# Query and key projections of the forgetting attention by Strassen's scheme in fp32, with bias spreads and key turns in one run among the products

## The chip, the cores and the metric

The kernel runs as one program on one core of a Trainium2 chip. The metric is the device time of one execution in microseconds; the figure that counts is the median over several executions. TensorE (PE in the rows) multiplies, VectorE (DVE), ScalarE (ACT) and GpSimd (POOL) do the elementwise work, and SyncE (SP) runs no arithmetic: it waits, reads indices and issues transfers, one after the other in program order. Each engine executes its own instruction list strictly in order, and the lists meet in semaphores.

## The reference, cut to what matters

One inference step of a one-layer decoder. A prompt of 1024 tokens and a sample group of 8 x 8 = 64 tokens go through the same weights, so that every projection is over 1088 tokens of 1024 channels. The part that is changed is the projection `fq`, `fk` below; beside it stand the load of `cache_fox_logf` through the page table, and the projections of the dilated heads (`dq`, `dk`, `dv`).

```python
def mixer_inputs(xn, pos, w_in, b_fgate):
    z = xn @ w_in
    fq, fk, fv, fz, dq, dk, dv, gate_fox, gate_dil = jnp.split(z, cuts, axis=-1)
    logf = jax.nn.log_sigmoid(fz.astype(jnp.float32) + b_fgate.astype(jnp.float32))
...
def fox_prompt(q, k, v, logf):            # 8 heads of 64, blocks of 128 queries
    c = jnp.cumsum(logf, axis=1)
    s = jnp.einsum('bqhd,bkhd->bhqk', qb, k) * (dh ** -0.5)
    s = s + cb[..., None] - c_keys[:, :, None, :]
    p = jax.nn.softmax(jnp.where(causal, s, -jnp.inf), axis=-1)
...
kv_past = cache_fox_kv[page_table, l]      # sample group: 16 pages of 128 rows for each of 8
lf_past = cache_fox_logf[page_table, l]
```

Everything is fp32. fk also leaves as an output, token by token.

## The kernel before, in words

`xnT` holds the normalised input with channels on partitions: 8 blocks (`KD`) of 128 channels by 1088 tokens. The weights `wK` and `wQ` hold 8 x 512 columns each. Two heads share 128 output columns; there are four such pairs, j = 0 to 3, in stages `p0` to `p3` of the plan. `foxpair_pe` makes, for a pair, the keys and the queries in chunks of 512, 288 and 288 tokens (`CHUNKS`): 8 matmuls into one of two PSUM banks, which ScalarE copies out to `KT` or `QT` (`foxpair_act`, semaphore `copied`). Each pair also needs four spreads of the cumulated log forgets over the partitions (512 columns each, "bias") and nine transposes of its keys ("turns", L561), which `foxpair_dve` copies from a third bank into one of two buffers `ktok`; POOL stores them (L637), and a buffer is taken again once its store has landed (`kstored0`, `kstored1`).

The order of each engine's list is not written down as such. Every stage is a generator that yields the planned time of its next step, and `weave` merges the generators of an engine by these times; the plan is the table `PLAN`, which the change leaves alone:

```python
PLAN = dict(
    norm1=(1.8, 73.8), v=(10, 82), p0=(82, 112), sums=(92, 93),
    p1=(112, 174), a0=(114, 176), p2=(174, 236), a1=(178, 238), p3=(236, 298), a2=(240, 300),
    d0=(298, 440), a3=(302, 372), b0=(380, 480), d1=(440, 580), b1=(500, 612), d2=(580, 715), b2=(640, 752),
```

The attention of pair j (`a0` to `a3`; scores L707, turns L735, values L724) is so laid among the projections of pair j + 1. `d0`, `d1` and `d2` are the projections of the three groups of dilated heads (`dilproj_pe`, matmuls L1068, turns L1085), with the attention `b0` of the first group (L838, L850, L863) beside `d1`. Their weights, 3 MB for a group in three transfers, are issued by SyncE in `dilproj_sp` (L1038), then a table of rotations (L1045). The past log forgets come by 128 transfers of 4 KB, whose addresses SyncE reads out of the page table one by one:

```python
for n in range(NB * NPG):                      # lf_sp, L1610 to L1615
    yield at("p0")(0) + 0.3 * n
    pid = sp.value_load(ptab[0:1, n:n + 1], min_val=0, max_val=N_POOL - 1)
    sp.dma_start(lf_raw[n:n + 1, :], lf_pool[bass.ds(pid, 1), :, :]...).then_inc(s_lf, 16)
```

They are transposed on TensorE in `p3` (L547), and `suffix_dve` sums them.

Of the kernel before, what the change touches and what calls it, by code (L numbers as in the profile page):

```python
# [22 lines left out]
P = 128  # L23
# [149 lines left out]
def build(nc, I, O, TAB):  # L173

    with ExitStack() as ctx:
# [225 lines left out]
        fp = sems("foxproj", "v_computed v_copied z_in z_act lf_out computed copied k_turned k_kept summed sums_out "  # L401
# [108 lines left out]
        PAIR_AT = [[sum(0.15 if kind == "bias" else 1.0 for kind, _ in units[0:x]) / 6.6 for x in range(PAIR + 1)]  # L510
                   for units in PAIR_UNITS]

        def foxpair_pe(pe, j):
            now = at(f"p{j}")
            for x, (kind, n) in enumerate(PAIR_UNITS[j > 0]):
                q, start = PAIR * j + x, PAIR_AT[j > 0][x]
                if kind == "bias":
                    yield now(start)
                    if j == 0 and n == 0:
                        pe.wait_ge(fp["sums_out"], 1)  # L520
                    pe.wait_ge(fp["copied"], q - 1)
                    pe.matmul(banks[q % 2], ident[:, 2 * j + n // 2:2 * j + n // 2 + 1].to_broadcast([P, P]),
                              cT[:, n % 2 * 512:(n % 2 + 1) * 512], start=True, stop=True).then_inc(fp["computed"], 1)
                    continue
                w, (c0, cw) = (wK if kind == "k" else wQ), CHUNKS[n]
                for k in range(KD):
                    yield now(start + k / KD / 6.6)
                    if k == 0 and q == 0:
                        pe.wait_ge(fp["wk_in"], 16)
                        pe.wait_ge(*nth(n1, "kept", 2 * TT))  # L530
                        conv_rows_pe(pe)
                    if k == 0 and q == 3:
                        pe.wait_ge(fp["wq_in"], 16)
                    if k == 0 and q >= 2:
                        pe.wait_ge(fp["copied"], q - 1)
                    last = pe.matmul(banks[q % 2][:, 0:cw], w[:, k, j * P:(j + 1) * P], xnT[:, k, c0:c0 + cw],  # L536
                                     start=(k == 0), stop=(k == KD - 1))
                last.then_inc(fp["computed"], 1)
                if kind == "k" and j == 3 and n < 2:
                    yield now(start + 0.95 / 6.6)  # L540
                    if n == 0:
                        pe.wait_ge(s_lf, 16 * NB * NPG)
                        pe.wait_ge(fp["k_kept"], 9)
                    else:
                        pe.wait_ge(fp["lf_kept"], 1)
                    for h in range(4):
                        last = pe.transpose(banks[2][:, h * P:(h + 1) * P], lf_raw[:, 4 * n + h::HF], ident)  # L547
                    last.then_inc(fp["lf_turned"], 1)
                if kind == "q":
                    g = 3 * j + n  # L550
                    yield now(start + 0.95 / 6.6)
                    pe.wait_ge(fp["copied"], PAIR * j + 3)
                    if g == 0:
                        pe.wait_ge(s_vec, 2)
                    else:
                        pe.wait_ge(fp["k_kept"], g)
                    if g == 9:
                        pe.wait_ge(fp["lf_kept"], 2)
                    for i in range(4 if n < 2 else 1):
                        t = 4 * n + i  # L560
                        last = pe.transpose(banks[2][0:rows_of(t), i * P:(i + 1) * P], KT[j % 2][:, t * P:t * P + rows_of(t)], ident)  # L561
                    last.then_inc(fp["k_turned"], 1)

        def foxpair_act(act, j):
            now = at(f"p{j}")
            for x, (kind, n) in enumerate(PAIR_UNITS[j > 0]):
                q = PAIR * j + x
                yield now(PAIR_AT[j > 0][x + 1])
                act.wait_ge(fp["computed"], q + 1)
                if x == 0 and j == 0:  # L570
                    act.wait_ge(*nth(n1, "kept", 2 * TT))
                    act.wait_ge(s_clear, 4)
                if x == 0 and j >= 2:
                    act.wait_ge(*nth(att_fox, "scored", att_fox["scored_by"][NQ * (j - 1) - 1]))
                    act.wait_ge(*nth(att_fox, "drained", att_fox["scored_by"][NQ * (j - 1) - 1]))
                    act.wait_ge(fp["k_turned"], 3 * (j - 1))
                src = banks[q % 2]
                if kind == "bias":
                    act.activation(bias_p[j % 2][:, n // 2, n % 2 * 512:(n % 2 + 1) * 512], src, ACT.Copy).then_inc(fp["copied"], 1)
                    continue  # L580
                c0, cw = CHUNKS[n]
                if kind == "k":
                    act.activation(KT[j % 2][:, c0:c0 + cw], src[:, 0:cw], ACT.Copy).then_inc(fp["copied"], 1)
                else:
                    m = min(cw, S - c0)
                    last = act.activation(QT[j % 2][:, c0:c0 + m], src[:, 0:m], ACT.Copy, scale=-QSCALE)
                    if m < cw:
                        for a in range(2):
                            last = act.activation(qbF[64 * a:64 * a + 64, j, :, 8 * a:8 * a + 8],
                                                  src[64 * a:64 * a + 64, m:cw].rearrange("p (b c) -> p b c", c=NS),  # L590
                                                  ACT.Copy, scale=QSCALE)
                    last.then_inc(fp["copied"], 1)

        def foxpair_dve(dve, j):
            now = at(f"p{j}")
            if j == 0:
                yield now(0.1)
                conv_rows_dve(dve)
            for n in range(2 if j == 3 else 0):
                yield now((n + 1.1) / 6.6)  # L600
                dve.wait_ge(fp["lf_turned"], n + 1)
                dve.tensor_copy(lf_all.rearrange("s p (b h) -> s h b p", h=HF)[:, 4 * n:4 * n + 4, :, :],
                                banks[2].rearrange("s (h b p) -> s h b p", h=4, b=NB)).then_inc(fp["lf_kept"], 1)
            for n in range(3):
                yield now(PAIR_AT[j > 0][PAIR_UNITS[j > 0].index(("q", n)) + 1])
                g, r = 3 * j + n, (P, P, SM)[n]
                dve.wait_ge(fp["k_turned"], g + 1)
                if g >= 2:
                    dve.wait_ge(fp[f"kstored{g % 2}"], 16 * (g // 2))
                w = 512 if n < 2 else P  # L610
                dve.tensor_copy(ktok[g % 2][0:r, 0:w], banks[2][0:r, 0:w]).then_inc(fp["k_kept"], 1)
# [319 lines left out]
        def mask_rows(dve, x):  # L931

            j, u = x // NQ, NQ - 1 - x % NQ
            if u == NQ - 1:
                dve.wait_ge(fp["copied"], PAIR * (j + 1))
            v = bias_p[j % 2][:, :, u * P:(u + 1) * P]
            dve.tensor_tensor(v, v, causal.unsqueeze(1).to_broadcast([P, 2, P]), ALU.add).then_inc(fp["masked"], 1)

        def fox_unit(x):
            j, u = x // NQ, NQ - 1 - x % NQ  # L940

            def add_ready(dve):
# [5 lines left out]
                W=(u + 1) * P, scores_ready=lambda pe: pe.wait_ge(fp["copied"], PAIR * (j + 1)), add_ready=add_ready,  # L948
# [74 lines left out]
        def dilproj_sp(sp, g):  # L1023
            yield at(f"d{g}")(0) - 40 if g else at("p3")(0.6)
            if g == 0:
                sp.wait_ge(s_foxout, FOXOUT)
                sp.wait_ge(fp["lf_out"], 1)
                sp.wait_ge(fp["computed"], 4 * PAIR - 3)
# [11 lines left out]
            if g == 0:  # L1040
                yield at("p3")(1)
                sp.wait_ge(fp["computed"], 4 * PAIR)
# [4 lines left out]
        def dilproj_pe(pe, g):  # L1047
# [29 lines left out]
        def dil_turn(pe, g, t):  # L1077
            s, z = dp[g]["s"], dp[g]["z"]
            pe.wait_ge(s["roped"], z["roped"] + t + 1)
            if g == 0 and t == 0:  # L1080
                pe.wait_ge(fp["k_kept"], 12)
            if g or t:
# [43 lines left out]
        def dilproj_act(act, g):  # L1126
            s, z = dp[g]["s"], dp[g]["z"]
            now = at(f"d{g}")
            for t in range(TT + 1):
# [3 lines left out]
                if t < TT:  # L1133
                    if t == 0:
                        yield now(1 / TT)
                        if g == 0:
                            act.wait_ge(fp["computed"], 4 * PAIR)
# [470 lines left out]
        def lf_sp(sp):  # L1608

            for n in range(NB * NPG):  # L1610
                yield at("p0")(0) + 0.3 * n
                if n == 0:
                    sp.wait_ge(s_ptab, 16)
                pid = sp.value_load(ptab[0:1, n:n + 1], min_val=0, max_val=N_POOL - 1)
# [157 lines left out]

        def suffix_dve(dve):
            yield at("p3")(0.5)
            dve.wait_ge(fp["lf_kept"], 2)
            dve.memset(lfs[:, NPG - 1, :], 0.0).then_inc(fb["suffix"], 1)
            for n, p in enumerate(range(NPG - 2, -1, -1)):
                yield at("p3")(0.5) + 4 * n
# [1698 lines left out]
```

## Time and profile before

| | |
|---|---|
| three executions | 2625.26, 2626.5, 2635.47 us, median 2626.5 us |
| profiled execution | 2628.53 us, its span 2626.7 us |
| TensorE busy | 2591.1 us, 99% of the span |
| VectorE, ScalarE, GpSimd busy | 1195.6, 521.2, 178.4 us |
| granted TensorE clock, mean | 0.997 |
| moved by DMA | 299.22 MB |

The span is that of one execution; 1.8 us of its time lie outside. Busy TensorE includes the tail of each matmul, which overlaps the next one, so that lengths are better read from the starts of consecutive rows. One fp32 matmul is recorded as two instructions, a transpose as one.

### The profile page before, as it was taken

To read this page: it belongs to the slowest core of one execution; us is meant where nothing else is said; L and a number is where in the kernel's file an instruction comes from. 1 tells how busy PE (TensorE), PEld (TensorE's weight loads), DVE (VectorE), ACT (ScalarE), POOL (GpSimd) and SP (SyncE) were. 2 spreads that over 40 slices of the span, in tenths; PEclk is the share of its full clock that TensorE was granted. 3 is DMA by queue.
4 is the path that set the end of the run, shared out by engine and by line. 5 is a ranking of instruction groups with operands and counts; after the bars stand their busy time and mean duration, and the time that the engine had idled before them with its cause. 6 is when DMAs were issued, how large, how long until landed. Compare 5 with 4: busy or idle time off the path is not lost.

```text
span 2626.7 us, 37785 instructions
## 1 busy us (share of the span) xinstructions
PE 2591.1 (99%) x14338; PEld 1821.2 (69%) x14338; DVE 1195.6 (46%) x2902; ACT 521.2 (20%) x1143; POOL 178.4 (7%) x284
## 2 busy tenths in 40 slices
PE   8999999999999999999999999999999999999999
PEld 7655656666656666676445886558888888888887
DVE  2155653332253333343553443355666666654432
ACT  2233323221202222121011112311211212110002
POOL 1000001232202222000000000000000000000000
PEclk9999999999999999999999999999999999999999
DMA  5000101100117888787215104433544452162101
GB/s 199 23 13 10 62 1 58 62 20 21 49 29 232 267 260 259 233 267 238 111 48 202 42 1 165 153 82 116 185 142 136 148 163 68 33 202 94 66 31 69
DMA packets 208474, 299.22 MB, mean 114 GB/s; under 512 B 20941, under 2 KB 145246, under 8 KB 207254
## 3 DMA queue, kind: packets, MB, share of 16 engines
q1 hardware_dynamic: 149462, 192.47, 22.5%
q10 hardware_dynamic: 42976, 89.26, 10.6%
q0 software_dynamic: 15856, 15.07, 2.3%
q8 instruction: 115, 1.88, 0.3%
q14 instruction: 65, 0.53, 0.1%
HBM read 270.43 MB, written 65.71 MB: 128 GB/s over the span
## 4 chain that ended last, share of the span: by engine, by line
PE 95%; DMA 2%; DVE 1%; ACT 1%; ACTq 1%; issue 1%; SPq 0%; DVEq 0%
PE psum L2853 22%; PE psum L3235 11%; PE psum L1068 10%; PE psum L2048 8%; PE psum L536 5%; PE psum L2136 4%; PE psum L2535 4%; PE psum L1424 3%; PE psum L2237 3%; PE psum L2056 3%; PE psum L707 3%; PE psum L724 2%; PE psum L2513 2%; PE psum L1440 2%; PE psum L1460 2%; PE psum L735 1%
## 5 line engine op out<-in xcount | busy, mean ns | idle before, releaser
L2853 PE MATMUL psum<-arena 128*128 128x272 f32 x2464 | 568.0, 394 | 1.2 <-DVE arena L2927 1.2
L2853 PEld LDWEIGHTS psum<-arena 128*128 128x128 f32 x2464 | 469.9, 191 | 98.6 <-issue 1.3
L3235 PE MATMUL psum<-arena 128*128 128x256 f32 (+1 forms) x1584 | 288.1, 356 | 0.0
L1068 PE MATMUL psum<-arena 128*128 128x512 f32 (+3 forms) x960 | 284.6, 458 | 0.0
L2048 PE MATMUL psum<-arena 128*128 128x368 f32 (+1 forms) x768 | 279.1, 475 | 0.9 <-DVE arena L1984 0.6
L3235 PEld LDWEIGHTS psum<-arena 128*128 128x128 f32 (+1 forms) x1584 | 252.4, 178 | 34.7 <-issue 3.2
L1068 PEld LDWEIGHTS psum<-arena 128*128 128x128 f32 (+1 forms) x960 | 150.2, 179 | 89.1 <-issue 78.3
L2048 PEld LDWEIGHTS psum<-arena 128*128 128x128 f32 x768 | 127.8, 190 | 52.0 <-issue 14.8
L2956 DVE TENSOR_TENSOR arena<-arena,psum 128x272 f32<-128x272 f32 (+2 forms) x330 | 111.8, 378 | 112.7 <-PE psum L2853 112.0
L1424 PEld LDWEIGHTS psum<-arena 128*128 128x128 f32 x848 | 105.0, 141 | 69.1 <-issue 46.3
L2977 DVE SCALAR_TENSOR_TENSOR arena<-arena 128x1024 f32<-128x1024 f32 x88 | 113.1, 1285 | 52.6 <-ACT arena L2879 51.1
L2877 ACT ACTIVATE arena<-arena 128x1024 f32<-128x1024 f32 x44 | 54.2, 1232 | 401.2 <-DVE arena L2956 401.2
L536 PE MATMUL psum<-arena 128*128 128x288 f32 (+1 forms) x384 | 132.4, 478 | 0.2
L1483 DVE COPY arena<-psum 128x512 f32<-128x512 f32 (+1 forms) x108 | 73.6, 682 | 128.0 <-PE psum L1424 127.8
L1424 PE MATMUL psum<-arena 128*128 128x128 f32 x848 | 127.5, 273 | 3.0 <-DMA arena<-in_cache_fox_kv 1.8
L3347 DVE TENSOR_TENSOR arena<-arena,psum 128x256 f32<-128x256 f32 (+1 forms) x128 | 46.6, 401 | 178.9 <-PE psum L3235 178.8
L2136 PE MATMUL psum<-arena 128*128 128x512 f32 x256 | 122.0, 596 | 0.0
L1490 ACT ACTIVATE arena<-psum 128x512 f32<-128x512 f32 (+1 forms) x108 | 63.6, 589 | 293.4 <-PE psum L1424 290.2
L2535 PE MATMUL psum<-arena 128*128 128x272 f32 x448 | 108.2, 392 | 0.0
L2056 PE MATMUL psum<-arena 128*128 128x352 f32 (+2 forms) x288 | 100.8, 457 | 0.0
L784 DVE CUSTOM_DVE_ANT_0 arena<-psum,arena 128x512 f32<-128x512 f32 (+3 forms) x128 | 65.2, 538 | 75.5 <-PE psum L707 75.3
L2237 PE MATMUL psum<-arena 128*128 128x512 f32 x224 | 98.0, 593 | 0.8 <-issue 0.8
(274 smaller groups left out, 2950.6 us busy)
## 6 DMA issues: line engine op xcount, KB each, us to landing
arena<-in_cache_fox_kv ACTq DMA_DIRECT2D x128, 256.0 KB, 4.7
arena<-in_cache_fox_kv SPq DMA_DIRECT2D x128, 256.0 KB, 5.0
out_win_s<-in_cache_win_kv ACTq DMA_DIRECT2D x8, 4080.0 KB, 15.0
arena<-in_w_up SPq DMA_DIRECT2D x44, 512.0 KB, 6.5
arena<-in_w_down SPq DMA_DIRECT2D x14, 1408.0 KB, 6.2
arena<-in_cache_win_kv SPq DMA_DIRECT2D x16, 1024.0 KB, 8.6
arena<-in_cache_mem_kv SPq DMA_DIRECT2D x16, 1024.0 KB, 6.3
out_y_p<-arena SPq DMA_DIRECT2D x20, 512.0 KB, 2.7
```

What stands on the lines that cost most here:

```text
L536: last = pe.matmul(banks[q % 2][:, 0:cw], w[:, k, j * P:(j + 1) * P], xnT[:, k, c0:c0 + cw], start=(k == 0), stop=(k == KD - 1))
L1068: last = pe.matmul(banks[c0 // 512][p0:p0 + r, 0:n], xn_tile(k, g, t), wD[g][:, k, w0:w0 + n], start=(k == 0), stop=(k == KD - 1))
L1424: last = pe.transpose(a["turn"][n % 2][:, x * P:(x + 1) * P], k, ident)
L2048: last = pe.matmul(banks[0][:, 0:cw], w[:, k, :], xnT[:, k, c0:c0 + cw], start=(k == 0), stop=(k == KD - 1))
L2056: last = pe.matmul(banks[1][:, 0:pw], w[:, 8 + k, :], oT[:, k, c0:c0 + pw], start=(k == 0), stop=(k == kn - 1))
L2136: last = pe.matmul(banks[h], lhs(k)[:, t * P:(t + 1) * P], w[h][:, k, :], start=(k == 0), stop=(k == KD - 1))
L2237: last = pe.matmul(mix_out(u), merged[:, ks, tok + t * P:tok + (t + 1) * P][:, k, :], wm[side][:, ws, :][:, k, :], start=(k == 0), stop=(k ...
L2535: last = pe.matmul(query_bank(n), w[:, k, :], r[:, k, XT4 * p:XT4 * p + XT4], start=(k == 0), stop=(k == 3))
L2853: last = pe.matmul(bank_of(j, x, p), w[:, k, :], r[:, k, Q4 * p:Q4 * p + Q4], start=(k == 0), stop=(k == 3))
L2956: last = dve.tensor_tensor(dst, dst if base is None else view(base), view(bank), ALU.add)
L2977: dve.scalar_tensor_tensor(out=tp, in0=up[:, tap:tap + S], scalar=w, in1=tp, op0=ALU.mult, op1=ALU.add).then_inc(done, 1)
L3235: last = pe.matmul(down_out(u)[p0:p0 + r, 0:n], hT(f)[:, tok + t * P:tok + t * P + r], slot[slots[c]][:, f - fa, c0:c0 + n], start=(f == f ...
```

## The change

With the channels in two halves and the tokens in two halves of 544, the keys and queries of a pair are a product of 2 x 2 blocks: weights (key, query) by channel halves, inputs (channel halves) by token halves. Strassen's scheme (in Winograd's form) makes it from 7 block products in place of 8. Each product is done in two parts of 272 tokens (p = 0, 1), with 4 matmuls of 272 columns each, in one of three banks that go round. The first product is copied out by ScalarE; the others are added by VectorE onto `KT`, `QT` and one intermediate (`onto`). VectorE also makes the input sums `k_t1` to `k_t4` once, and the weight sums of each pair. The four spreads and the nine key turns of the pair ahead now use the same three banks and stand behind the eighth product part; the key turns of pair 3 come behind all products. `k_t1` takes the place of `lf_all` and `lf_raw`: so the loop of the past log forgets moves behind the last product, their transposes into `d1`.

```diff
-        PAIR = 10
-        ks, qs, bs = [("k", n) for n in range(3)], [("q", n) for n in range(3)], [("bias", n) for n in range(4)]
-        PAIR_UNITS = (ks + qs + bs, ks + bs + qs)
+        QT2, QT4 = TOK // 2, TOK // 4
+        SUMS, COPIES = 16, 7
+        PRODUCTS = [("product", x, p) for x in range(7) for p in range(2)]
+        SPREADS = [("bias", n, 0) for n in range(4)]
+        K_TURNS = [("turn", n, 0) for n in range(3)]
+        PAIR_UNITS = [PRODUCTS + SPREADS]
+        PAIR_UNITS += [PRODUCTS[0:8] + SPREADS + K_TURNS + PRODUCTS[8:] for j in range(3)]
+        PAIR_UNITS += [K_TURNS]
...
+        k_t1, k_t2, k_t3 = [take(4 * QT2, a).rearrange("p (k t) -> p k t", k=4) for a in (B2 + 4 * TOK, f0 + 34432, f0 + 15872)]
...
+            w = (a11, s2, a12, a21, a22, s1, s4)[x]
+            return w[:, k, :], t4 if x == 4 else (k_b11, k_t2, k_b21, k_t3, None, k_t1, k_b22)[x][:, k, cols]
...
-                w, (c0, cw) = (wK if kind == "k" else wQ), CHUNKS[n]
-                for k in range(KD):
...
-                    last = pe.matmul(banks[q % 2][:, 0:cw], w[:, k, j * P:(j + 1) * P], xnT[:, k, c0:c0 + cw],
-                                     start=(k == 0), stop=(k == KD - 1))
+                if kind == "turn":
+                    yield pair_at(j, i)
+                    pe.wait_ge(*nth(qk, "summed", SUMS * j))
+                    pair_drained(pe, q - 3)
...
+                for k in range(4):
+                    yield pair_at(j, i) + (pair_at(j, i + 1) - pair_at(j, i)) * k / 4
...
+                        if q >= 3:
+                            pair_drained(pe, q - 3)
+                    w, r = pair_operands(j, x, k, p)
+                    last = pe.matmul(banks[q % 3][:, 0:QT4], w, r, start=(k == 0), stop=(k == 3))
...
+        def pair_weight_sums(dve, j):
...
+            dve.tensor_tensor(s1, a21, a22, ALU.add).then_inc(qk["s"]["w_sums"], 1)
...
+                    if g >= 2:
+                        dve.wait_ge(fp[f"kstored{g % 2}"], 16 * (g // 2))
+                    dve.tensor_copy(ktok[g % 2][0:r, 0:w], banks[q % 3][0:r, 0:w]).then_inc(fp["k_kept"], 1)
...
-            yield at(f"d{g}")(0) - 40 if g else at("p3")(0.6)
+            yield at(f"d{g}")(0) - 40 if g else at("p3")(0.9)
...
-                sp.wait_ge(fp["computed"], 4 * PAIR - 3)
+                sp.wait_ge(*nth(qk, "computed", unit_at(3, "product", 4, 1) + 1))
...
-                                pe.wait_ge(fp["copied"], 4 * PAIR - (0 if c0 else 1))
+                                pe.wait_ge(*nth(qk, "summed", 4 * SUMS))
+                                pe.wait_ge(fp["k_kept"], 12)
...
         def lf_sp(sp):
 
             for n in range(NB * NPG):
-                yield at("p0")(0) + 0.3 * n
+                yield at("p3")(1) + 4 + 0.3 * n
                 if n == 0:
                     sp.wait_ge(s_ptab, 16)
+                    sp.wait_ge(*nth(qk, "computed", PAIR_FROM[4]))
...
+        def lf_turn_at(n):
+            return at("d1")(0) + 5 + 7 * n
```

What this does to SyncE's list. Before, the loop of 128 loads (each a read of the page table, L1614, and a transfer, L1615) stands ahead of all weights of the dilated projections:

```order
L1606 DMA ptab<-in_page_table 1x128
L1614 TENSOR_LOAD ptab [waits page_table_loaded]
L1614 ISA x2
L1615 ISA
L1615 DMA arena<-in_cache_fox_logf 1x1024
...
L1038 DMA arena<-in_w_in 128x8x256 [waits foxproj_computed,foxproj_lf_out,fox_outputs_stored]
L1038 DMA arena<-in_w_in 128x8x256 x2
L1045 DMA arena<-tab_rope 128x576 [waits foxproj_computed]
L1038 DMA arena<-in_w_in 128x8x256 [waits dil_computed,att_taken,dil_roped,att_kept_odd,att_kept_even]
L1038 DMA arena<-in_w_in 128x8x256 x2
```

Of the changed kernel, from the same row on (L1208 is L1038 of before, L1215 is L1045, L1789 and L1790 are L1614 and L1615):

```order
L1780 DMA ptab<-in_page_table 1x128
L1208 DMA arena<-in_w_in 128x8x256 [waits quarters_computed,quarters_summed,foxproj_lf_out,fox_outputs_stored]
L1208 DMA arena<-in_w_in 128x8x256 x2
L1215 DMA arena<-tab_rope 128x576 [waits quarters_computed]
L1789 TENSOR_LOAD ptab [waits quarters_computed,page_table_loaded]
L1789 ISA x2
L1790 ISA
L1790 DMA arena<-in_cache_fox_logf 1x1024
...
L1208 DMA arena<-in_w_in 128x8x256 [waits dil_computed,att_taken,dil_roped,att_kept_odd,att_kept_even]
L1208 DMA arena<-in_w_in 128x8x256 x2
```

The 128 loads have moved from ahead of the weights of group 0 to between the weights of group 0 and those of group 1.

TensorE's list at the seam of `p3` and `d0`, before (L536 the projections of pair 3, L561 the last key turn, L1068 the first matmul of `d0`):

```order
L724 MATMUL psum<-arena 64x128 x5
L536 MATMUL psum<-arena 128x288
L561 MATMUL psum<-arena 64x128 [waits foxproj_k_kept,foxproj_copied]
L1068 MATMUL psum<-arena 128x512 [waits foxproj_copied,dil_w_in]
L735 MATMUL psum<-arena 128x128 [waits att_kept_even,att_normed]
```

and of the changed kernel (L628 the products, L603 the key turns, L1239 the matmuls of `d0`):

```order
L628 MATMUL psum<-arena 128x272
L603 MATMUL psum<-arena 128x128 [waits quarters_summed]
L603 MATMUL psum<-arena 128x128 x3
L900 MATMUL psum<-arena 128x128 [waits att_kept_even,att_normed]
L900 MATMUL psum<-arena 128x128 x3
L603 MATMUL psum<-arena 128x128 [waits quarters_summed]
L603 MATMUL psum<-arena 128x128 x3
L603 MATMUL psum<-arena 64x128 [waits quarters_summed]
L1239 MATMUL psum<-arena 128x512 [waits foxproj_k_kept,quarters_summed,dil_w_in]
```

Eight of the nine key turns of pair 3 have moved behind the last product, and the first matmul of `d0` now waits for their copies as well.

TensorE's list where `d1` begins, before:

```order
L1085 MATMUL psum<-arena 128x128
L1068 MATMUL psum<-arena 128x512 [waits dil_roped,ring_landed8,dil_w_in]
L1068 MATMUL psum<-arena 128x512 x7
L863 MATMUL psum<-arena 128x128 [waits att_expd,att_kept_even]
L863 MATMUL psum<-arena 128x128 x3
```

and of the changed kernel (L1259 the last turn of `d0`, L1960 the transposes of the past log forgets):

```order
L1259 MATMUL psum<-arena 128x128
L1239 MATMUL psum<-arena 128x512 [waits dil_roped,ring_landed8,dil_w_in]
L1239 MATMUL psum<-arena 128x512 x4
L1960 MATMUL psum<-arena 128x128 [waits dil_kept,past_log_forgets_loaded]
L1960 MATMUL psum<-arena 128x128 x3
L1239 MATMUL psum<-arena 128x512 x3
```

The eight transposes of the past log forgets now stand inside the first tile of `d1`, four and four, and nothing else has moved there.

## Rows read from the trace of the kernel before

**Rows 1.** The page: busy time, then 40 slices of the span with TensorE's granted clock.

```profile
PE 2591.1 (99%) x14338; PEld 1821.2 (69%) x14338; DVE 1195.6 (46%) x2902; ACT 521.2 (20%) x1143; POOL 178.4 (7%) x284
PE   8999999999999999999999999999999999999999
PEclk9999999999999999999999999999999999999999
```

**Rows 2.** A stretch, busy us of each engine (instructions), clock, DMA share, GB/s.

```profile
115.00:315.00 200.00, 197.66 (x1133) 117.27 (x1132) 109.80 (x330) 71.99 (x165) 6.25 (x9) 1.00 0.09 27
```

**Rows 3.** Timeline of TensorE in p0: start, length, instructions in a row.

```profile
81.06 11.98 PE L536 MATMUL psum<-arena 128*128 128x512 f32 x36
...
106.67 4.05 PE L536 MATMUL psum<-arena 128*128 128x288 f32 x16
110.55 0.60 PE L561 MATMUL psum<-arena 128*128 128x128 f32 x4
110.98 4.05 PE L536 MATMUL psum<-arena 128*128 128x288 f32 x16
```

**Rows 4.** Timeline of TensorE, a run of 272 columns in the MLP.

```profile
1879.68 20.56 PE L2853 MATMUL psum<-arena 128*128 128x272 f32 x89
```

**Rows 5.** VectorE's instruction groups by form: busy, mean ns, idle before.

```profile
L2956 DVE TENSOR_TENSOR arena<-arena,psum 128x272 f32<-128x272 f32 x198 | 80.5, 435 | 76.7 <-PE psum L2853 75.9
L2942 DVE TENSOR_TENSOR arena<-arena 128x512 f32<-128x512 f32 x22 | 15.2, 692 | 0.8
```

**Rows 6.** Timeline of VectorE in p0.

```profile
75.14 0.42 DVE L342 TENSOR_TENSOR arena<-psum,arena 128x256 f32<-128x256 f32 x1 [1.92 <-PE psum L371]
...
85.51 1.18 DVE L487 TENSOR_TENSOR arena<-arena 128x8 f32<-128x8 f32 x6
```

**Rows 7.** Line L637, POOL's stores of turned keys.

```profile
L637 POOL DMA_DIRECT2D out_fox_kv_p<-arena x8: 752/771/801, 107.8 to 306.7; - x8
DMA to landing us min/median/max: 1.8/2.7/3.1
```

**Rows 8.** Timeline of SyncE's transfers.

```profile
282.21 2.32 SPq L1038 DMA_DIRECT2D arena<-in_w_in  x3
314.36 0.35 SPq L1045 DMA_DIRECT2D arena<-tab_rope  x1
403.40 2.23 SPq L1038 DMA_DIRECT2D arena<-in_w_in  x3
```

**Rows 9.** Lines L1614 and L1615, SyncE: ns min/median/max, first and last start us.

```profile
L1614 SPq TENSOR_LOAD <-ptab x128: 472/492/803, 46.7 to 207.4; - x128
L1615 SPq DMA_DIRECT2D arena<-in_cache_fox_logf x128: 254/255/289, 47.7 to 208.3; - x128
```

**Rows 10.** Timeline of SyncE, loads of past keys and values, addresses read likewise.

```profile
793.15 36.30 SPq L1649 DMA_DIRECT2D arena<-in_cache_fox_kv  x25
```

**Rows 11.** Stretches around the weights of group 1 (columns as in rows 2).

```profile
412.00:414.00 2.00, 2.00 (x14) 1.24 (x12) 0.00 (x0) 0.39 (x1) 0.00 (x0) 1.00 1.10 353
414.00:416.00 2.00, 2.00 (x17) 1.35 (x16) 1.71 (x10) 0.72 (x3) 0.00 (x0) 1.00 0.26 93
```

**Rows 12.** Timeline of TensorE where d1 begins.

```profile
456.05 7.03 PE L1068 MATMUL psum<-arena 128*128 128x512 f32 x16
462.92 1.04 PE L863 MATMUL psum<-arena 128*128 128x128 f32 x8
```

**Rows 13.** Timeline of TensorE at the start of the program.

```profile
7.37 0.56 PE L277 MATMUL psum<-arena 8*128 8x8 f32 x4 [7.37 <-DMA arena<-in_g_ffn]
...
14.32 1.06 PE L437 MATMUL psum<-arena 128*128 128x256 f32 x2
15.18 1.07 PE L438 MATMUL psum<-arena 128*128 128x264 f32 x2
16.06 0.62 PE L437 MATMUL psum<-arena 128*128 128x256 f32 x2
16.52 0.61 PE L438 MATMUL psum<-arena 128*128 128x264 f32 x2
```

More of the change, by code:

```diff
@@ new lines, in build @@
+        SPREADS = [("bias", n, 0) for n in range(4)]
[3 more added lines that the diff above has]
+        PAIR_UNITS += [K_TURNS]
+        COST = {"product": 1.0, "bias": 0.5, "turn": 0.25}
+        PAIR_FROM = [sum(len(u) for u in PAIR_UNITS[0:j]) for j in range(6)]
+        PAIR_AT = [[sum(COST[u[0]] for u in units[0:x]) / 16.75 for x in range(len(units) + 1)] for units in PAIR_UNITS]
@@ new lines, in build, with pair_block, pair_sums @@
+        k_t4 = take(3 * QT2, f0 + 15872 + 4 * QT2).rearrange("p (k t) -> p k t", k=3)
+        k_t4_last = [take(QT4, a) for a in (f0 + 15872 + 7 * QT2, f0 + 34432 + 4 * QT2)]
+        assert 15872 + 7 * QT2 + QT4 <= 20032 and 34432 + 4 * QT2 + QT4 <= 36896
+        q_new = [spare[:, SM * i:SM * i + SM] for i in range(2)]
+        def pair_block(w, j, half):
+            return w[:, 4 * half:4 * half + 4, j * P:(j + 1) * P]
+        def pair_sums(j):
+            if j == 0:
+                return [take(512, f0 + 1024 + 512 * i).rearrange("p (k n) -> p k n", k=4) for i in range(3)]
+            return [pair_block(wK, j - 1, 0), pair_block(wK, j - 1, 1), pair_block(wQ, j - 1, 0)]
@@ new lines, in pair_u2, with pair_operands @@
+        def pair_u2(j, p):
+            if j == 3:
+                return k_t2[:, 0, QT4 * p:QT4 * p + QT4]
+            return take(QT4, (f0 + 2560 if j == 0 else f0 + 20248) + QT4 * p)
+        def pair_operands(j, x, k, p):
+            a11, a12, a21, a22 = [pair_block(w, j, half) for w in (wK, wQ) for half in range(2)]
+            s1, s2, s4 = pair_sums(j)
+            cols = slice(QT4 * p, QT4 * p + QT4)
+            t4 = k_t4[:, k, cols] if k < 3 else k_t4_last[p]
+            w = (a11, s2, a12, a21, a22, s1, s4)[x]
+            return w[:, k, :], t4 if x == 4 else (k_b11, k_t2, k_b21, k_t3, None, k_t1, k_b22)[x][:, k, cols]
@@ L538, in foxpair_pe @@
[L538 to L562, printed above, removed]
@@ L564, in foxpair_act @@
-        def foxpair_act(act, j):
[L565 to L570, printed above, removed]
+                if kind == "turn":
+                    yield pair_at(j, i)
+                    pe.wait_ge(*nth(qk, "summed", SUMS * j))
+                    pair_drained(pe, q - 3)
+                    for n in range(4 if x < 2 else 1):
+                        t = 4 * x + n
+                        last = pe.transpose(banks[q % 3][0:rows_of(t), n * P:(n + 1) * P],
+                                            KT[(j - 1) % 2][:, t * P:t * P + rows_of(t)], ident)
+                    last.then_inc(qk["s"]["computed"], 1)
+                    continue
@@ L571, in foxpair_act @@
+                last.then_inc(qk["s"]["computed"], 1)
+        def foxpair_act(act, j):
+            for i, (kind, x, p) in enumerate(PAIR_UNITS[j]):
+                q = PAIR_FROM[j] + i
+                if kind == "turn" or kind == "product" and x:
+                    continue
+                yield pair_at(j, i + 1)
+                act.wait_ge(*nth(qk, "computed", q + 1))
+                if i == 0 and j == 0:
                     act.wait_ge(*nth(n1, "kept", 2 * TT))
                     act.wait_ge(s_clear, 4)
[L573 to L576, printed above, removed]
@@ L594, in foxpair_dve @@
[L594 to L611, printed above, removed]
+                if i == 0 and j >= 2:
+                    pairs_read(act, j)
```

243 lines of the change are left out of this document (200 added, 43 removed).

## The prediction

> **What bounds the kernel now.** I read the page first, for the engine that is never idle. TensorE is busy for 2591.1 of 2626.7 us, its granted clock is at the top in every slice, and VectorE, the next, has 46% [rows 1]. So the time is the length of TensorE's list, plus the stretches in which it waits; work on other engines costs nothing until TensorE waits for it. Then I read the stretch of pairs 1 to 3: of 200 us TensorE lacks 2.3, VectorE is busy for 109.8, ScalarE for 72.0 [rows 2]. The third view is the timeline of SyncE, since the change moves 128 of its transfers: where each load was issued, and when TensorE first used it [rows 8, 9, 12].
>
> **The products.** One fp32 matmul is two instructions here. From starts of consecutive rows, 16 instructions of 512 columns take 462.92 - 456.05 = 6.87 us, 0.429 each [rows 12]; 16 of 288 columns take 110.55 - 106.67 = 3.88 us, 0.2425 each; the row's own length, 4.05, has a tail of 0.17 [rows 3]. 89 of 272 columns take 20.56 us with that tail, so 0.229 each [rows 4]. A pair now costs 2 x (2 x 8) instructions of 512 and 4 x (2 x 8) of 288: 32 x 0.429 + 64 x 0.2425 = 29.25 us. Afterwards it costs 7 x 2 x 4 x 2 = 112 of 272: 25.65 us. The gain is 3.6 us for a pair, 14.4 us for four. The bounds are 13.5 us (with 0.231) and 14.7 us (7/8 of the old cost alone would give 3.66). Spreads and turns keep their number, so they cancel.
>
> **The sums.** Each pair gives VectorE 16 sums of 272 columns out of PSUM, two of which are cut in two, and four weight sums of 512. At 0.435 and 0.692 us [rows 5] that is about 7.3 + 2.8 = 10 us. Three pairs put 30 us onto the 109.8, so VectorE would be busy for about 75% of a stretch that has shrunk to some 189 us. ScalarE loses copies. On the average that is hidden; it can show where VectorE's list has a lump. I find three.
>
> First, p0. The second halves of the input sums can begin when the norm is done, at 75.14 + 0.42 [rows 6]. At 0.692 us for 512 elements, 1088 cost 1.4 us. In the order of VectorE's list: four input sums to 81.3, three weight sums to 83.4, the rows of the convolution (0.3), then 2.8 + 3.0 us of input sums and a weight sum of 0.7, to 90.2, the log forgets (1.2 in [rows 6], 1.4 with the step ahead) to 91.6; only then the first product is added, 92.0. TensorE takes the bank back with its sixth product part, 81.06 + 5 x 1.83 = 90.2. Stall: about 2 us. The weight sums are there in time (83.4 against 81.06 + 3.7).
>
> Second, the third key turn of a pair. Its copy waits until the store of the first has landed: copy 0.69, issue 0.77, landing 2.7 [rows 7], some 4.3 us after that turn. TensorE has about 4 us of other work in its list by then, so 0.5 to 1 us in each of p1 to p3, say 2.5 together. These stand ahead of the last product, with the 2 us of p0: 4.5 us. Nothing is the lower bound, 12 us the upper (1 us per weight-sum and turn lump, twelve of them).
>
> Third, the seam of p3 and d0: the key turns of pair 3 follow the last product at once (0.5 us for its sum), and `d0` waits for the third copy, which again waits for a store. TensorE has 1 us of other work against 4.7: a stall of about 4 us in all, 0 to 5.
>
> The weights of group 0 are issued later, behind product 4 of pair 3. Behind it come 16 product matmuls (32 x 0.229 = 7.3 us), 33 transposes (3.6 us by [rows 3]), and scores and values of the attention that I put at 4 us, some 15 us in all; the load takes 11 (below). It stays hidden.
>
> **The moved loads.** This is the term that decides. SyncE's loop costs per load a page-table read of 0.49 us, a transfer issue of 0.255 us and the register work between. The first read starts at 46.7, the last at 207.4, so 160.7 / 127 = 1.265 us per load; the whole is 208.6 - 46.7 = 161.9 us [rows 9]. Another loop of the same build takes 36.30 us for 25, 1.45 each [rows 10], so it is not the time of the transfer that sets the pace: the transfers are 64 times as large there. Before, the loop lay ahead of everything that SyncE had to issue, from 46.7 to 208.6, and the next issue was due at 282.21 [rows 8]. It was covered by 74 us of nothing to do. Afterwards it starts when the last product is computed, and the weights of group 1 stand behind it.
>
> When is the last product computed? The rotation table waited for the same point before, 314.36 [rows 8]. Minus 14.4, minus 16 transposes that now come later (eight of keys, eight of log forgets, at 0.43 us for four [rows 3], 1.7 us), plus 4.5 of stalls: 302.7. The table's issue takes 0.35, and the loop 161.9: the weights are issued at 465.0. Before, they were issued at 403.40 [rows 8], and the transfers ran at full share until 414 and for a quarter of the next 2 us [rows 11], so the load takes 11.1 us, and lands at 476.1. The first matmul of `d1` waits for it; it stood at 456.05 [rows 12], and TensorE would now come to it at 456.05 - 14.4 - 0.9 + 4.5 + 4 = 449.3 (the key turns are back in by then, the log forgets' transposes are not). It waits for 26.8 us. Behind it are queued all products of `d1` and the attention of group 0; TensorE has no other list.
>
> In the Trainium skill, DMA: Bandwidth & Descriptors, section Latency and other measured facts, a `tensor_load` is given a floor of about 600 ns. If that were the whole of the step, an estimate, 128 of them would be 77 us, the weights would be early, and the sum would be -14.4 + 4.5 + 4 = -5.9 us; the row has 0.49 us for the read and 1.265 for the step, so the trace decides against it.
>
> **The clock after the wait.** At the start of the program, after 7.37 us without a matmul, TensorE multiplies, and two instructions of 256 columns stand 0.87 us apart until 16.06, then 0.46 [rows 13]: the lower of its two levels (1.2 GHz), then the upper (2.4), though the granted clock reads 1.00. Half of those 8.7 us at most was lost, 4; I take 3 us after a wait of 27, bounds 1.5 and 4. The Trainium skill, TensorE: Matmul & The Clock Gate, Part 1, says that the slow state is the default and that activity releases it; the trace agrees at the start, and no row of before shows a wait of this length later on.
>
> **The sum.** -14.4 (products) + 4.5 (stalls ahead) + 4 (seam) + 26.8 (weights of group 1) + 3 (clock) = +23.9 us. The first and third terms are swallowed by the wait: the end moves with the landing, (476.1 - 456.05) + 0.9 + 3 = 24. Against the profiled execution (2628.53, that is span 2626.7 and 1.8 around it) it gives 2652.5, and against the median, which is 2.0 lower, 2626.5 + 24 = **2650.5 us**, 0.9% slower. Nothing later gives it back, since TensorE is as full to the end.
>
> **The rivals.**
> 1. *The loop costs TensorE nothing* (it runs faster, or the weights land early enough). It would have to take 1.05 us per load or less: (449.3 - 11.2 - 303.1) / 128. Then the sum is -5.9, 2620.5 us; with no stall at all -14.4, 2612 us, and only this end is faster by over 0.5%. For it: the read and the issue are only 0.75 us of a step of 1.265 [rows 9]. Against: 1.265 and 1.45 in two places, with a queue otherwise empty. Chance 0.06, of which 0.03 for the end below -0.5%.
> 2. *VectorE becomes the bound in the products.* At 75% and in order, with attention sums that TensorE waits for in the same list. If each lump costs 1 us, the products end 7.5 us later, the loop starts 7.5 us later, and the time is 2658; if VectorE lacks 10%, some 20 us, the time is 2670. Before, TensorE lost only 2.3 us there, at 55%. Chance 0.10.
> 3. *A part of the wait is filled or made up*: no stalls ahead (-4.5), and the clock hardly falls (-2). Then 2644; with a loop of 1.18 us (10.9 us less), 2639, which is the limit of 0.5%, 13 us. Chance 0.08, half of it below that limit.
>
> **How the numbers follow.** The forecast has 0.76. Its own range, with stalls ahead from 0 to 8 and the clock from 1.5 to 4, is 2644 to 2656. To hold 8 in 10 with the rivals on both sides it reaches from 2641 to 2661. A measurement of this kernel tells about 0.5%, 13 us, from no change. Slower by more: 0.76 + 0.10 + 0.04 = 0.90. Within: 0.03 + 0.04 = 0.07. Faster: 0.03.
>
> **What would show it.** In the profile of the changed kernel: the products at 0.229 us spacing; the last one at about 303 us; SyncE's loop from there to about 465, 1.265 us a load; the next transfers at 465; TensorE idle for some 27 us ahead of the first matmul of `d1`, released by the weights, its first rows behind at double spacing; VectorE about 30 us busier in pairs 1 to 3. The prediction is wrong if the loop is shorter than 140 us, or if TensorE's idle time before 300 us is over 12 us.

## The result

The changed kernel takes 2644.01 us (median of 4 executions, 2642.97 to 2651.21), the kernel before 2625.88 us (median of 4). The ratio is 1.0067, with a 95% interval from 1.0037 to 1.0097: 18 us slower. The forecast was 2650.5 us, its range 2641 to 2661. Measured again on the chip of the later experiments, against 17 executions of the kernel before, the same kernel came to 1.0048 (1.0035 to 1.0061). The profiled execution took 2642.97 us with a span of 2641.2 us, against 2628.53 and 2626.7.

The page after: TensorE's busy time has fallen by 11.4 us, and still the span is 14.5 us longer (compare [rows 1]). Two slices, the seventh and eighth (396 to 528 us), are below 9, which they were not before.

```profile
PE 2579.7 (98%) x14402; PEld 1835.3 (69%) x14402; DVE 1238.5 (47%) x2999; ACT 514.6 (19%) x1127; POOL 178.0 (7%) x284
PE   8999997899999999999999999999999999999999
```

The table of TensorE's waits, whole program, longest first (engine, line, what ended the wait: us in total, times, longest), says where. The first and third rows are new; before, no wait of TensorE between 81 and 640 us was over 0.9 us.

```profile
PE psum L1239 <- DMA arena<-in_w_in: 23.8, 1, 23.8
PE psum L277 <- DMA arena<-in_g_ffn: 7.5, 1, 7.5
PE psum L1239 <- DVE arena L737: 3.3, 1, 3.3
PE psum L371 <- DVE arena L356: 2.1, 2, 1.8
PE psum L900 <- DVE arena L910: 1.8, 4, 0.6
```

SyncE's timeline of the changed kernel answers [rows 8]. The rotation table goes out with the last product, at 297.98 (before: 314.36). Then 128 loads keep SyncE for 159.78 us, and the weights of group 1 are issued at 459.38 in place of 403.40.

```profile
283.00 2.21 SPq L1208 DMA_DIRECT2D arena<-in_w_in  x3
297.98 0.35 SPq L1215 DMA_DIRECT2D arena<-tab_rope  x1
299.40 159.78 SPq L1790 DMA_DIRECT2D arena<-in_cache_fox_logf  x128
459.38 2.21 SPq L1208 DMA_DIRECT2D arena<-in_w_in  x3
```

Both seams on TensorE's timeline of the changed kernel (answering [rows 12] at the second). At the first, the key turns (L603) follow the last product, then the first matmul of `d0` stands still for 3.33 us. At the second, the last turn of `d0` is issued at 446.29, and the first matmul of `d1` at 470.57, released by its weights.

```profile
297.22 0.73 PE L628 MATMUL psum<-arena 128*128 128x272 f32 x2
298.48 0.66 PE L603 MATMUL psum<-arena 128*128 128x128 f32 x4 [0.53 <-DVE arena L723]
298.98 0.60 PE L900 MATMUL psum<-arena 128*128 128x128 f32 x4
299.41 0.71 PE L603 MATMUL psum<-arena 128*128 128x128 f32 x5
303.46 5.37 PE L1239 MATMUL psum<-arena 128*128 128x512 f32 x8 [3.33 <-DVE arena L737]
...
446.29 0.44 PE L1259 MATMUL psum<-arena 128*128 128x128 f32 x2
470.57 6.34 PE L1239 MATMUL psum<-arena 128*128 128x512 f32 x10 [23.84 <-DMA arena<-in_w_in]
```

Read the lengths too: 8 instructions of 512 columns in 5.37 us and 10 in 6.34 are some 0.67 and 0.63 us each, where 16 took 7.03 us before, 0.44 each. The stretches show the granted clock (last column but two): half behind either wait, full again within 5 us. Behind the longer wait this costs about 2 us, and about as much behind the shorter.

```profile
304.00:308.00 4.00, 4.00 (x7) 1.58 (x6) 0.18 (x1) 0.00 (x0) 0.15 (x1) 0.63 0.05 12
308.00:312.00 4.00, 4.00 (x11) 1.36 (x10) 1.31 (x4) 0.00 (x0) 0.00 (x0) 1.00 0.01 4
...
454.00:470.00 16.00, 0.00 (x0) 0.00 (x0) 0.00 (x0) 0.00 (x0) 2.47 (x6) 0.50 0.66 207
470.00:475.00 5.00, 4.43 (x6) 1.92 (x7) 0.00 (x0) 0.00 (x0) 0.00 (x0) 0.58 0.10 36
475.00:480.00 5.00, 5.00 (x18) 2.53 (x17) 1.06 (x1) 0.00 (x0) 0.00 (x0) 1.00 0.00 0
```

The lag of the changed kernel behind the old one, from the starts of the same instructions in the two traces, adds up as follows:

| place | before | after | difference |
|---|---|---|---|
| SyncE sees the last product | 314.36 | 297.98 | -16.4 |
| first matmul of `d0` | 314.3 | 303.5 | -10.8 |
| first matmul of `d1` | 456.05 | 470.57 | +14.5 |
| first matmul behind `d2` (L2048) | 682.0 | 699.3 | +17.3 |
| first matmul of the MLP (L2853) | 1755.2 | 1769.7 | +14.5 |
| span | 2626.7 | 2641.2 | +14.5 |

The first -16.4 holds 16 transposes that have moved behind this point (1.7 us), so the products gave 14.7 us. (The first product itself stands 0.4 us later than the first projection matmul of before, at 81.45 against 81.06; counted from there it is 15.1.) The 2.8 us given back between 682 and 1755 are taken up at the end.

### The profile page after: what moved, and what is told of

It is laid out like the page before. It is cut to its first block, busy times and chain, and to the rows that moved or that the text cites. A ratio compares the mean times of both kernels' runs of the same rounds, so it can differ in the third digit from the quotient of the medians.

```text
span 2641.2 us, 38053 instructions
## 1 busy us (share of the span) xinstructions
PE 2579.7 (98%) x14402; PEld 1835.3 (69%) x14402; DVE 1238.5 (47%) x2999; ACT 514.6 (19%) x1127; POOL 178.0 (7%) x284
## 4 chain that ended last, share of the span: by engine, by line
PE 89%; SPq 5%; issue 2%; DMA 2%; DVE 1%; ACTq 1%; ACT 0%; DVEq 0%
PE psum L3050 21%; PE psum L3432 11%; PE psum L2245 8%; PE psum L1239 7%; PE psum L2333 4%; PE psum L628 4%; PE psum L2732 4%; PE psum L1598 3%; SPq L1789 3%; PE psum L2434 3%; PE psum L2253 3%; PE psum L872 2%; PE psum L2710 2%; PE psum L889 2%; PE psum L1614 2%
## 5 line engine op out<-in xcount | busy, mean ns | idle before, releaser
L3050 PE MATMUL psum<-arena 128*128 128x272 f32 x2464 | 567.9, 394 | 1.2 <-DVE arena L3124 1.2
L3050 PEld LDWEIGHTS psum<-arena 128*128 128x128 f32 x2464 | 469.9, 191 | 98.6 <-issue 1.3
L1239 PE MATMUL psum<-arena 128*128 128x512 f32 (+3 forms) x960 | 288.5, 462 | 27.2 <-DMA arena<-in_w_in 23.8
L2245 PE MATMUL psum<-arena 128*128 128x368 f32 (+1 forms) x768 | 279.1, 475 | 1.2 <-DVE arena L2181 0.7
L1239 PEld LDWEIGHTS psum<-arena 128*128 128x128 f32 (+1 forms) x960 | 151.4, 181 | 118.8 <-issue 84.1
L2245 PEld LDWEIGHTS psum<-arena 128*128 128x128 f32 x768 | 127.8, 190 | 52.3 <-issue 14.8
L1598 PEld LDWEIGHTS psum<-arena 128*128 128x128 f32 x848 | 105.1, 141 | 68.9 <-issue 46.0
L628 PE MATMUL psum<-arena 128*128 128x272 f32 x448 | 116.2, 400 | 0.0
L2732 PE MATMUL psum<-arena 128*128 128x272 f32 x448 | 108.2, 392 | 0.0
L628 PEld LDWEIGHTS psum<-arena 128*128 128x128 f32 x448 | 80.1, 190 | 25.3 <-issue 12.1
```

The lines of the kernel that those rows point to most:

```text
L628: last = pe.matmul(banks[q % 3][:, 0:QT4], w, r, start=(k == 0), stop=(k == 3))
L1239: last = pe.matmul(banks[c0 // 512][p0:p0 + r, 0:n], xn_tile(k, g, t), wD[g][:, k, w0:w0 + n], start=(k == 0), stop=(k == KD - 1))
L1598: last = pe.transpose(a["turn"][n % 2][:, x * P:(x + 1) * P], k, ident)
L2245: last = pe.matmul(banks[0][:, 0:cw], w[:, k, :], xnT[:, k, c0:c0 + cw], start=(k == 0), stop=(k == KD - 1))
L2732: last = pe.matmul(query_bank(n), w[:, k, :], r[:, k, XT4 * p:XT4 * p + XT4], start=(k == 0), stop=(k == 3))
L3050: last = pe.matmul(bank_of(j, x, p), w[:, k, :], r[:, k, Q4 * p:Q4 * p + Q4], start=(k == 0), stop=(k == 3))
```

## The experiments

The theory (A): SyncE's list is serial, its loop of page-table reads costs 1.25 us a load, and the weights of group 1 now queue behind it; what the products save is lost in that wait. Rivals: the products' overlap gives nothing by itself (B), the small transfers and not the reads set the loop's pace (C), the waits add up independently (D); two more that a single run names are E (the loads ahead of the weights overlap with them, and do not count one by one) and F (VectorE is at the edge). Ratios are to the kernel before on the same chip. The 120 loads, the changed kernel again and the last two kernels were measured on one chip, the other four on another.

**The split loop.** All work is kept. The plan spaces the loads so that 78 stand ahead of the weights of group 1 and 50 behind; the log forgets' transposes move behind the first turn of `d1`.

```diff
-                yield at("p3")(1) + 4 + 0.3 * n
+                yield at("p3")(1) + 4 + 1.265 * n
...
-            return at("d1")(0) + 5 + 7 * n
+            return at("d1")(0) + 34 + 6 * n
...
-                    pe.wait_ge(*nth(dp[0], "kept", TT))
+                    pe.wait_ge(*nth(dp[1], "kept", 1))
```

The wait on `lf_kept` also moves from tile 0 to tile 1 of `d1`.

> The changed kernel with one thing altered: the plan spaces the 128 loads of the past log forgets by 1.265, so that SyncE issues the weights of group 1 behind the first 78 of them; the transposes of the log forgets move to behind the first turn of d1. All work is kept. Theory A (the loop ahead of the weights costs TensorE the 23.8 us wait, 2 us of clock behind it): the wait is gone, the seam wait of 3.3 us stays, the time is 2644 - 26 = 2618 us, some 8 us under the kernel before (0.3%). Theory B (the products save nothing once they overlap, and TensorE waits elsewhere when this wait is taken away): 2632 or more.

Measured: 2620.66 us, ratio 0.9951 (0.9936 to 0.9967). Its SyncE timeline:

```profile
299.70 97.11 SPq L1790 DMA_DIRECT2D arena<-in_cache_fox_logf  x78
397.01 2.59 SPq L1208 DMA_DIRECT2D arena<-in_w_in  x3
399.64 2.72 SPq L1215 DMA_DIRECT2D arena<-tab_rope  x1
403.30 62.01 SPq L1790 DMA_DIRECT2D arena<-in_cache_fox_logf  x50
```

and TensorE at the second seam, with no wait and 16 instructions of 512 columns in 7.03 us, as before the change:

```profile
446.61 0.44 PE L1259 MATMUL psum<-arena 128*128 128x128 f32 x2
446.88 7.03 PE L1239 MATMUL psum<-arena 128*128 128x512 f32 x16
```

The order of two things in SyncE's list turns a loss of 0.5 to 0.7% into a gain of 0.5%. The transposes have moved too, but the kernel without table reads (below) leaves them in the first tile of `d1`, and its wait is gone as well. B is out: this kernel has every product and every sum of the changed one, and is under 2632. It reaches the stage behind `d2` at 673.7, against 682.0 before and 699.3 after.

**The late loop alone.** The old projections; of the change only the late loop and the transposes in `d1`.

```diff
         def lf_sp(sp):
...
-                yield at("p0")(0) + 0.3 * n
+                yield at("p3")(1) + 4 + 0.3 * n
                 if n == 0:
                     sp.wait_ge(s_ptab, 16)
+                    sp.wait_ge(fp["computed"], 4 * PAIR)
```

> The kernel before, with its old projections, and of the change only the move of the loop behind the last projection and of the log forgets' transposes into d1. All work is kept. Theory A: the loop runs from about 313 to 474 us, the weights of group 1 land at about 485, TensorE comes to them at 456 and waits for 29 to 30 us, then 2 us of slow clock: 2626 + 31 = 2657 us (1.2% slower than before, and about 13 us slower than the changed kernel, since the loop begins later by what the products save). Theory B (the wait belongs to the products): no wait, within 3 us of 2626.

Measured: ratio 1.0111 (1.0094 to 1.0129), 31 us by the medians (2663.76 against 2632.43), as expected. The loop runs from 315.69 for 159.79 us, the weights are issued at 475.69, and the wait is there with no Strassen product in the kernel:

```profile
455.69 0.44 PE L1070 MATMUL psum<-arena 128*128 128x128 f32 x2
487.19 5.10 PE L1051 MATMUL psum<-arena 128*128 128x512 f32 x6 [31.06 <-DMA arena<-in_w_in]
```

`d1` begins 16.6 us later than in the changed kernel (470.57), nearly the 16.3 us by which the loop began later (315.69 against 299.40). So this is how the products' gain still reaches the end of the program: through the start of the loop. By the ratios this kernel is 0.4 to 0.6% slower than the changed one (12 to 17 us), where 13 us were expected.

**No read of the page table.** The changed kernel with the 128 loads at fixed addresses, pages 0 to 127: the read and the indirection are left out, the transfers stay.

```diff
-                pid = sp.value_load(ptab[0:1, n:n + 1], min_val=0, max_val=N_POOL - 1)
-                sp.dma_start(lf_raw[n:n + 1, :], lf_pool[bass.ds(pid, 1), :, :]...
+                sp.dma_start(lf_raw[n:n + 1, :], lf_pool[n:n + 1, :, :]...
```

> The changed kernel, but the 128 loads take pages 0 to 127 at fixed addresses: the reads of the page table are left out, so that the past log forgets are those of other pages; as many bytes in as many transfers. Theory A (the sequencer's read and register work set the pace): the step falls from 1.25 to about 0.4 us, the loop ends at about 350 us, no wait ahead of d1, time about 2618 us. Theory C (the small transfers themselves set the pace): the step stays at 1.25 us and the time at 2644.

Measured: 2620.87 us, ratio 0.9954 (0.9940 to 0.9968), and no wait for the weights. The same 128 transfers now take SyncE 38 us, 0.30 each where 0.4 was expected, so C is out; reads, register work and the dispatch between them are 0.95 of the 1.25 us.

```profile
297.26 38.02 SPq L1789 DMA_DIRECT2D arena<-in_cache_fox_logf  x128
393.61 2.46 SPq L1208 DMA_DIRECT2D arena<-in_w_in  x3
```

**120 loads ahead.** As the split loop, spaced by 0.8167, so that 120 loads precede the weights.

```diff
-                yield at("p3")(1) + 4 + 1.265 * n
+                yield at("p3")(1) + 4 + 0.8167 * n
```

> As the kernel with the split loop, but 120 loads in place of 78 stand ahead of the weights of group 1. All work is kept. Theory A (past the point where the weights are late, each load ahead of them costs its 1.25 us): the weights are issued at 298.4 + 120 x 1.25 = 448.4 us, land at 459.6, TensorE comes at 446.6 and waits for 13 us, loses about 2 us of clock behind it, and the kernel takes 15 us more than the one with the split loop (ratio to before about 1.001). Theory E (the step's cost is not linear, and the loads overlap the weights): less than half of that.

Measured: ratio 1.0030 (1.0020 to 1.0040), 0.0079 above the split loop (which was measured on the other chip), where 0.006 was expected. The wait came out as worked out, and the changed kernel, with 8 more loads ahead of the weights, begins `d1` 9.6 us later (470.57), 1.2 for each load. E is out:

```profile
447.47 0.44 PE L1259 MATMUL psum<-arena 128*128 128x128 f32 x2
460.99 5.49 PE L1239 MATMUL psum<-arena 128*128 128x512 f32 x6 [13.08 <-DMA arena<-in_w_in]
```

By the ratio the time lies some 5 us above the forecast for this kernel, though the wait is as forecast; by the medians of the two chips it is 3 (2638.33 against 2620.66 + 15). In the traces the stage behind `d2` begins 17.1 us later than with the split loop (690.8 against 673.7), where 15 were forecast. Slow clock is 2.2 us of that: behind the same seam wait of 3.3 us it cost 3.2 us here and 1.8 there, and behind the long wait 2.8 where 2 were expected. What the ratio has above these 17.1 us is open.

**A third buffer.** The changed kernel with a small buffer of its own for the 64-row key turn, whose copy then waits for no store of the same pair.

```diff
-        ktok = [take(512, f0 + 6656 + 512 * i) for i in range(2)]
+        ktok = [take(512, f0 + 6656 + 512 * i) for i in range(2)] + [spare[:, 128:256]]
...
-                    if g >= 2:
-                        dve.wait_ge(fp[f"kstored{g % 2}"], 16 * (g // 2))
+                    if g >= 3:
+                        dve.wait_ge(fp[f"kstored{x}"], 16 * (g // 3))
```

> The changed kernel with a third, small buffer for the 64-row key turn, so that its copy no longer waits for the store of the first turn of the pair. All work is kept. Theory A (the end of the program hangs on the loop, which starts at the last product): the seam wait of 3.3 us before d0 mostly goes, TensorE comes to d1 some 3 to 5 us earlier and waits for as much longer (about 28 us), and the time stays within 2 us of 2644. Theory D (the waits add up): 2639 to 2640.

Measured: ratio 1.0051 (1.0032 to 1.0071), against 1.0048 and 1.0067 of the changed kernel itself: nothing gained. These intervals are too wide to tell the 4 to 5 us of D from nothing; the trace tells them. Its table of waits has the 2 us of the seam back at the next one, and 2 more that the clock had cost behind it:

```profile
PE psum L1239 <- DMA arena<-in_w_in: 27.7, 1, 27.7
...
PE psum L1239 <- DVE arena L737: 1.3, 1, 1.3
```

TensorE comes to `d1` 4.1 us earlier than in the changed kernel (its last turn of `d0` is issued at 442.21, against 446.29) and begins it at 470.36, against 470.57. D is out: what TensorE saves between the last product and `d1` is waited off there.

**The changed kernel again,** on the chip of the kernel with 120 loads ahead and of the two that follow.

> The changed kernel itself, on the same chip as the three kernels below, so that they can be set against it. Both theories: the ratio to the kernel before that it had the first time, 1.0067, within its interval.

Measured: ratio 1.0048 (1.0035 to 1.0061). It lies within the interval of the first time, and the two intervals overlap, but the 1.0067 of the first time is just outside this one. The wait for the weights is 24.4 us here.

**Split loop and third buffer.** Both edits together.

> The split loop (78 loads ahead of the weights) together with the third, small buffer for the 64-row key turn. All work is kept. Theory A: with no wait behind it that hides it, the seam wait now counts: 3.4 us becomes about 1.3, and the clock does not fall behind it, which saves some 2 us more: 4 us under the kernel with the split loop (ratio to before about 0.9935). Theory D (the seam does not matter here either): equal to it, 0.995.

Measured: ratio 0.9948 (0.9933 to 0.9962). With the long wait gone the seam counts in the trace: the stage behind `d2` begins at 668.7, 5.0 us ahead of the kernel with the split loop alone. Of these, 1.2 were there at the last product (297.04 against 298.28), 0.9 of them already at the first (80.84 against 81.76), ahead of anything that the edit touches; 3.8 come behind it, with the seam, near the 4 of theory A. In whole executions the two are not told apart (0.9951 and 0.9948, on two chips, and the interval holds both forecasts, 0.9935 and 0.995), so a gain of the buffer in time is not shown. It has the lowest ratio of all, 0.5% under the kernel before, but three versions lie within 0.1% of each other.

**Longer lumps on VectorE.** On top of the last, the first weight sum of each pair is made five times over, 11 us more for VectorE in all.

```diff
+            for i in range(4):
+                dve.tensor_tensor(s1, a21, a22, ALU.add).then_inc(s_extra, 1)
+                dve.wait_ge(s_extra, 4 * j + i + 1)
             dve.tensor_tensor(s1, a21, a22, ALU.add).then_inc(qk["s"]["w_sums"], 1)
```

> As the kernel with split loop and third buffer, and the first weight sum of each pair is made five times over, so that VectorE has 4 x 0.69 = 2.8 us more in a lump for each of the four pairs, 11 us in all; the result is unchanged. Theory A (VectorE's lumps are hidden by the three banks and the attention between): TensorE waits for 1 to 3 us more in all, and the time is within 4 us of the kernel without. Theory F (VectorE is at the edge, as my upper bound for the waits had it): 8 us or more.

Measured: ratio 0.9969 (0.9956 to 0.9981), 6 us by the medians above the kernel without. Theory A said within 4 us, F said 8 or more, so neither was right in size. The waits that are new in it (81 to 116 us, then 180 to 305; another of 1.2 us behind L914 lies between them):

```profile
PE psum L629 <- ACT arena L648: 1.4, 1, 1.4
PE psum L629 <- DVE arena L295: 1.1, 1, 1.1
PE psum L629 <- DVE arena L725: 0.3, 1, 0.3
...
PE psum L893 <- DVE arena L914: 1.4, 1, 1.4
```

Together they are 5.4 us, where theory A had 1 to 3. The last product is seen 7.5 us later (304.51 against 297.04); the first product already stands 1.0 us later (81.82 against 80.84), ahead of any extra sum. So about half of the 11 us put onto VectorE comes out of TensorE. As many sums as the change has are hidden, but the cover in p0 is thin: 2.8 us more there bring waits of 2.8 us at once.

## Why the prediction was right

*The products* (-14.4): right. 16.4 us less 1.7 for moved transposes is 14.7, the upper of the bounds given (which, at 7/8 of 29.25 us a pair, comes to 14.6). From first product to last it is 15.1, of which 0.3 is less waiting.

*The stalls ahead of the last product* (+4.5): over-sized, and the one term that moved the forecast. The trace has no new wait in p0, and from 115 to 297 us TensorE lacks 2.1 us where the old kernel lacked 2.3. In p0 the working had 1.4 us for an input sum of 1088 elements, scaled up from one of 512; the sum takes 1.28, as the timeline of VectorE in the changed kernel shows, and the first product is added at 90.31 where I had 92, while TensorE began 0.4 us later than the 81.06 of the working.

```profile
75.86 1.28 DVE L662 TENSOR_TENSOR arena<-arena 128x1088 f32<-128x1088 f32 x1
77.18 1.29 DVE L664 TENSOR_TENSOR arena<-arena 128x1088 f32<-128x1088 f32 x1
...
83.49 2.48 DVE L671 TENSOR_TENSOR arena<-arena 128x1088 f32<-128x1088 f32 x2
...
90.31 0.78 DVE L754 TENSOR_TENSOR arena<-arena,psum 128x272 f32<-128x272 f32 x2
```

The other part, 2.5 us for the third key turn of a pair, came to nothing. VectorE did wait for the stores ahead of its copy, 7.1 us at the four third turns together (L737), 2.0 of them at the seam; in p1 to p3 TensorE had other work for as long, and none of its waits there is for a key turn. The load on VectorE was as forecast: from 115 to 297 us it is busy for 128.0 us, before for 97.9.

*The seam* (+4): 0.5 and 3.3 us of waiting, and 2 us of slow clock behind it, which the sum did not have. It did not matter for the end, as the text said, and the third buffer showed.

*The weights of group 0* stayed hidden: issued at 283.00, and no wait for them.

*The loop* (26.8 us of wait): right in mechanism and nearly in size, 23.8. SyncE's loop took 161 us with its first read, as forecast; it started 4.7 us earlier, since the 4.5 us of stalls were not there, and so the wait ended at 470.6 and not at 476.1. It was shorter by 3 and not by 5.5 since TensorE came 2.7 us earlier too.

*The clock* (+3): 2 us behind the wait, at the lower level of 1.2 GHz from before the first matmul to about 474.5. The Trainium skill, TensorE: Matmul & The Clock Gate, Part 1, as cited there, has activity release the slow state. The trace agrees behind this wait, and here the profile's granted clock shows it as 0.50, which it did not at the start of the program.

*The rivals.* The loop did not run faster than 1.05 us a load, VectorE did not become the bound, and nothing that was foreseen filled the wait. With 4.5 off, 24 becomes 19.5, against 18.1 by the medians, 17.3 behind `d2` in the two traces, and 14.5 between their spans.

## What to carry to other kernels

A step that only waits, reads indices and issues is work too: 128 loads with a table read each cost SyncE 160 us, and they were free only while nothing else was due in its list. When data changes places in memory and a loop of loads must move with it, count the loop by its own rate and look at what is queued behind it, not at its bytes (0.5 MB here). And where such a wait swallows every gain between the loop's start and its end, mend that first; until then only what moves the start of the loop reaches the end of the program.

## What the runs showed of the hardware

Short waits cost twice, but not always. Behind a wait of 3.3 us at the first seam the granted clock fell to half and TensorE lost about 2 us, and 3.2 us behind the same wait in the trace with 120 loads ahead; with the third buffer the wait there was 1.3 us, and the clock stayed at 1.00.

More surprising is a stretch near 1260 us, in which no instruction was changed. Two executions of the same changed kernel are at the same point at 699.3 us (the first of L2245) and within 1.3 us at 1255 (its last), but 6.6 us apart at the start of the MLP. Of the first profile:

```profile
1262.00:1268.00 6.00, 6.00 (x56) 6.00 (x56) 0.33 (x1) 0.00 (x0) 0.00 (x0) 1.00 0.81 309
1268.00:1274.00 6.00, 5.17 (x14) 2.62 (x14) 1.38 (x2) 0.00 (x0) 0.00 (x0) 0.72 0.44 148
```

and of the second, in which the clock is at half for some 20 us, and 96 matmuls of 64 columns (L2267) take 18.6 us in place of 10.9, though TensorE has an instruction running nearly all the time:

```profile
1256.00:1262.00 6.00, 5.47 (x36) 5.50 (x36) 1.22 (x3) 0.00 (x0) 0.00 (x0) 0.74 1.04 387
1262.00:1268.00 6.00, 6.00 (x30) 6.00 (x30) 0.19 (x1) 0.00 (x0) 0.00 (x0) 0.50 0.59 227
1268.00:1274.00 6.00, 6.00 (x30) 6.00 (x30) 0.00 (x0) 0.00 (x0) 0.00 (x0) 0.50 0.00 0
1274.00:1280.00 6.00, 5.17 (x12) 2.77 (x12) 1.38 (x2) 0.00 (x0) 0.00 (x0) 0.55 0.41 113
```

The trace with the third buffer alone has the same fall, at the same matmuls (17.8 us between the first and the last of them, against 10.7). The executions of these kernels spread by 3 to 14 us, and this stretch can be a good part of it: of the changed kernel, those of 2643 to 2644 us have a mean granted clock of 0.992 or 0.993, that of 2651.21 has 0.989, as has the second profiled one, 2649.53. What sets it off was not tried. It is also where the changed kernel got its 2.8 us back: in the profile of before, a wait of 3.0 us at 1269 is followed by half clock until about 1276, and in that of after the wait ahead of the same instruction (at 1287) is 1.8 us and no fall follows it. The fall to 0.72 in the first profile above is a shorter one, ahead of that wait.
